# Ninety-six convolution taps on VectorE alone, in a two-layer encoder on one core

## The reference, cut to what matters

```python
def conformer_conv(u, dw_w, dw_b, norm_g, norm_b):
    a, gate = jnp.split(u, 2, axis=-1)
    z = a * jax.nn.sigmoid(gate)
    z = lax.conv_general_dilated(
        z, dw_w[:, None, :].astype(z.dtype), window_strides=(1,),
        padding=[(CONV_PAD, CONV_PAD)], dimension_numbers=('NWC', 'WIO', 'NWC'),
        feature_group_count=CONV_CH) + dw_b      # CONV_CH = 512, 31 taps wide
    z = layer_norm(z, norm_g, norm_b)
    return jax.nn.silu(z)

def attn_conv_mixer(...):
    ...
    attn = block_attention(q, k, v)              # 8 heads, softmax over 512 keys
    conv = conformer_conv(u, dw_w, dw_b, conv_norm_g, conv_norm_b)
    return jnp.concatenate([attn, conv], axis=-1) @ w_out
```

## Time and profile before

| | us |
|---|---|
| median of 3 runs | 1434.68 (1434.39 to 1436.61) |
| the profiled execution, its own time | 1434.18 |
| its span | 1432.4 |
| PE busy | 1383.2 (97%) |
| DVE busy | 664.6 (46%) |
| ACT busy | 459.6 (32%) |
| POOL busy | 221.6 (15%) |

### The profile page before, as it was taken

The page is one execution under the profiler, slowest core; times in us unless marked ns, Lnnn a source line. Parts: engine busy times, 40 slices in busy tenths (PEclk is TensorE's granted clock), DMA queues, the critical chain, the costliest instruction groups (busy, mean ns, idle before and its releaser), DMA issues.

```text
span 1432.4 us, 16564 instructions
## 1 busy us (share of the span) xinstructions
PE 1383.2 (97%) x6684; PEld 1162.5 (81%) x6684; DVE 664.6 (46%) x823; ACT 459.6 (32%) x552; POOL 221.6 (15%) x194
## 2 busy tenths in 40 slices
PE   7969789999999999999999999999999999999997
PEld 7757677888888888889888888888888888888886
DVE  4669893733333322166555453654373333332225
ACT  3357553332232221133232332423233222322211
POOL 5279851300000000033201002000030000000000
PEclk9989999999999999999999999999999999999999
DMA  6200001223222332303231212222222233224221
GB/s 213 89 30 1 30 30 59 89 88 109 96 88 94 109 120 88 115 33 137 67 105 59 88 59 88 89 89 89 88 89 88 88 99 106 88 89 146 88 89 59
DMA packets 84015, 124.15 MB, mean 87 GB/s; under 512 B 2688, under 2 KB 61312, under 8 KB 83968
## 3 DMA queue, kind: packets, MB, share of 16 engines
q1 hardware_dynamic: 83968, 123.49, 25.7%
HBM read 121.39 MB, written 2.10 MB: 86 GB/s over the span
## 4 chain that ended last, share of the span: by engine, by line
PE 86%; DVE 6%; POOL 4%; ACT 2%; issue 1%; DMA 0%; POOLq 0%; DVEq 0%; SPq 0%; ACTq 0%
PE ps L1236 22%; PE ps L1238 22%; PE ps L1237 22%; PE ps L1312 19%; DVE acc L914 2%; POOL acc L501 2%; POOL w_lo L377 1%; PE ps L1249 1%; ACT w_hi L373 1%; DVE row_max L1000 1%; DVE probT_lo L1017 1%; PE ps L1522 0%; PE ps L1442 0%; DMA x_tok<-in_x 0%; DVE x_tok L1059 0%
## 5 line engine op out<-in xcount | busy, mean ns | idle before, releaser
L377 DVE TENSOR_TENSOR w_lo<-raw,w_hi 128x2048 fp32r<-128x2048 f32 x101 | 231.8, 2295 | 487.1 <-ACT w_hi L373 487.1
L1236 PE MATMUL ps<-xT_hi,w_hi 128*128 128x512 f32 (+1 forms) x992 | 366.6, 370 | 0.5 <-POOL w_lo L377 0.5
L1237 PE MATMUL ps<-xT_lo,w_hi 128*128 128x512 f32 (+1 forms) x992 | 365.5, 368 | 0.0
L1238 PE MATMUL ps<-xT_hi,w_lo 128*128 128x512 f32 (+1 forms) x992 | 365.5, 368 | 0.0
L373 ACT ACTIVATE w_hi<-raw 128x2048 fp32r<-128x2048 f32 x109 | 208.4, 1912 | 429.7 <-PE ps L1238 251.1
L1236 PEld LDWEIGHTS ps<-xT_hi,w_hi 128*128 128x128 f32 x992 | 186.9, 188 | 32.1 <-POOL w_lo L377 1.1
L1238 PEld LDWEIGHTS ps<-xT_hi,w_lo 128*128 128x128 f32 x992 | 186.9, 188 | 31.4
L1237 PEld LDWEIGHTS ps<-xT_lo,w_hi 128*128 128x128 f32 x992 | 187.0, 188 | 31.2
L575 POOL TENSOR_SCALAR var_eps<-var_eps 128x1 f32<-128x1 f32 x16 | 5.6, 352 | 846.9 <-ACT squares L768 846.9
L1236 PE MATMUL ps<-w_hi,xT_hi 128*128 128x512 f32 (+1 forms) x320 | 121.3, 379 | 0.0
L1237 PE MATMUL ps<-w_lo,xT_hi 128*128 128x512 f32 (+1 forms) x320 | 121.1, 378 | 0.0
(11 more groups left out here) (167 smaller groups left out, 1760.8 us busy)
## 6 DMA issues: line engine op xcount, KB each, us to landing
raw<-in_l_w_in SPq DMA_DIRECT2D x31, 1024.0 KB, 5.2
raw<-in_l_ffn_w_gate SPq DMA_DIRECT2D x22, 1024.0 KB, 5.1
raw<-in_l_ffn_w_up SPq DMA_DIRECT2D x22, 1024.0 KB, 5.1
raw<-in_l_ffn_w_down SPq DMA_DIRECT2D x22, 1024.0 KB, 4.7
raw<-in_l_w_out SPq DMA_DIRECT2D x12, 1024.0 KB, 4.9
x_tok<-in_x SPq DMA_DIRECT2D x4, 512.0 KB, 7.2
out<-x_tok SPq DMA_DIRECT2D x8, 256.0 KB, 2.1
ln_gb<-in_l_ln_mix_g SPq DMA_DIRECT2D x2, 512.0 KB, 5.2
```

Source lines behind the costliest of these rows:

```text
L377: eng.tensor_tensor(w_lo[ch.s][:], raw[ch.s][:], f32(w_hi[ch.s][:]), ALU.subtract)\
L1236: nc.tensor.matmul(dst, a[0], b[0], start=start, stop=False)
L1237: nc.tensor.matmul(dst, a[0], b[1], start=False, stop=False)
L1238: return nc.tensor.matmul(dst, a[1], b[0], start=False, stop=stop)
```

## The change

All 47 taps that ScalarE and GpSimd shared become VectorE's. `tap_products`, `add_taps`, the buffers `tap_part` and `side_sum` and their semaphores go. VectorE's list of taps is now tiles 0, 1 and 2 in full and the last three taps of tile 3: 96. Ahead of step 0 it does 1 + 19 + 4 of them, and then 3 in every step, which lasts to step 23. PE's wait for the additions in step 27 goes; its own instructions stay the same, in the same order.

```diff
--- before.py
+++ after.py
@@ -76,7 +76,6 @@
-HANDED = 16
...
@@ -87,13 +86,11 @@
-SIDE_SUM_STEP = 25
...
-DVE_TAPS = 2 * TAPS - HANDED + TAPS - BATCH * BATCHES
-ADDED = TAPS - 1 + HANDED - 1
+DVE_TAPS = 3 * TAPS + TAPS - BATCH * BATCHES
...
@@ -489,18 +482,6 @@
-            def add_taps(count):
-                for a in range(added[0], min(added[0] + count, ADDED)):
-                    own_tile = a < TAPS - 1
-                    total = acc[:, 1, :] if own_tile else side_sum[:]
-                    pool.wait_ge(part_tapped, a + (2 if own_tile else 3))
-                    if a:
-                        pool.wait_ge(part_added, a)
-                    nc.gpsimd.tensor_tensor(total, total, tap_part[:, a % 4, :], ALU.add).then_inc(part_added, 1)
-                    added[0] += 1
...
@@ -525,15 +506,9 @@
             for b in range(2):
                 diagonals(b)
-            add_taps(18)
 
             def attention_step(s):
                 b = s // 2
-                add_taps(1 + (s % 4 == 1))
-                if s == SIDE_SUM_STEP:
-                    pool.wait_ge(tap_done, 2 * TAPS - HANDED)
-                    pool.wait_ge(part_added, ADDED)
-                    nc.gpsimd.tensor_tensor(acc[:, 2, :], acc[:, 2, :], side_sum[:], ALU.add).then_inc(part_added, 1)
...
@@ -629,26 +604,6 @@
-            def tap_products(count):
-                for n in range(tapped[0], min(tapped[0] + count, TAPS + HANDED)):
-                    ct, k = (1, n) if n < TAPS else (2, n - HANDED)
-                    tap, z = conv_par[:, ct, k:k + 1], zpad[:, ct, k:k + SEQ]
...
-                        if a >= 4:
-                            act.wait_ge(part_added, a - 3)
-                        nc.scalar.activation(tap_part[:, a % 4, :], z, ACT.Copy, scale=tap).then_inc(part_tapped, 1)
...
@@ -690,9 +645,7 @@
             glu_sigmoid(1)
-            tap_products(16)
             glu_sigmoid(2)
-            tap_products(4)
             glu_sigmoid(3)
...
@@ -709,7 +662,6 @@
                 if s == 0:
                     z_tile_hi()
-                tap_products(1 + (s % 4 == 0))
...
@@ -896,8 +848,8 @@
-            taps = [(0, k) for k in range(TAPS)] + [(2, k) for k in range(TAPS - HANDED)] \
-                + [(3, k) for k in range(BATCH * BATCHES, TAPS)]
+            taps = [(ct, k) for ct in range(3) for k in range(TAPS)] + [(3, k) for k in range(BATCH * BATCHES, TAPS)]
...
@@ -988,9 +940,9 @@
             glu_product(1)
-            conv(9)
+            conv(19)
             glu_product(2)
-            conv(2)
+            conv(4)
...
@@ -1016,7 +968,7 @@
-                conv(2 - s % 2)
+                conv(3)
...
@@ -1447,7 +1399,6 @@
                         pe.wait_ge(tap_done, DVE_TAPS)
-                        pe.wait_ge(part_added, ADDED + 1)
                         pe.wait_ge(conv_copied, 1)
```

More of the change, by code:

```diff
@@ L164, in build_encoder @@
         k_turned = place("k_turned", [P, TT, KV * HD], F32, work + 22 * KB)
-        tap_part = place("tap_part", [P, 4, SEQ], F32, work + 24 * KB)
         qT_hi = place("qT_hi", [P, TT, 4, P], F32R, work + 32 * KB)
@@ L172, in build_encoder @@
         rope_gain = place("rope_gain", [P, TT, 2, 2, HD], F32, work + 68 * KB)
-        side_sum = place("side_sum", [P, SEQ], F32, work + 68 * KB)
         o_raw = [place(f"o_raw{i}", [P, GROUP, 2, HD], F32, work + at * KB) for i, at in enumerate((72, 78))]
@@ L249, in build_encoder @@
         tap_done = sem("tap_done")
-        part_tapped = sem("part_tapped")
-        part_added = sem("part_added")
         diag_made = sem("diag_made")
@@ L489, in _ @@
                             .then_inc(rope_gain_made, 1)
-            added = [0]
-            def add_taps(count):
-                for a in range(added[0], min(added[0] + count, ADDED)):
-                    own_tile = a < TAPS - 1
-                    total = acc[:, 1, :] if own_tile else side_sum[:]
-                    pool.wait_ge(part_tapped, a + (2 if own_tile else 3))
-                    if a:
-                        pool.wait_ge(part_added, a)
-                    nc.gpsimd.tensor_tensor(total, total, tap_part[:, a % 4, :], ALU.add).then_inc(part_added, 1)
-                    added[0] += 1
             for t in range(TT):
@@ L631, in _ @@
             make_hi(act, Chunk(C_Q))
-            tapped = [0]
-            def tap_products(count):
-                for n in range(tapped[0], min(tapped[0] + count, TAPS + HANDED)):
-                    ct, k = (1, n) if n < TAPS else (2, n - HANDED)
-                    tap, z = conv_par[:, ct, k:k + 1], zpad[:, ct, k:k + SEQ]
[L639 to L647, removed]
-                        if a >= 4:
-                            act.wait_ge(part_added, a - 3)
-                        nc.scalar.activation(tap_part[:, a % 4, :], z, ACT.Copy, scale=tap).then_inc(part_tapped, 1)
-                    tapped[0] += 1
             def glu_sigmoid(ct):
@@ L896, in xT_tile_lo @@
                                             f32(xT_hi[spot]), ALU.subtract).then_inc(xT_lo_made, 1)
-            taps = [(0, k) for k in range(TAPS)] + [(2, k) for k in range(TAPS - HANDED)] \
-                + [(3, k) for k in range(BATCH * BATCHES, TAPS)]
+            taps = [(ct, k) for ct in range(3) for k in range(TAPS)] + [(3, k) for k in range(BATCH * BATCHES, TAPS)]
+            assert len(taps) == DVE_TAPS
             tapped = [0]
```

## The result

The changed kernel takes 1447.33 us (median of 6 runs, 1446.52 to 1448.08), the kernel before 1435.51 in 6 runs (1434.39 to 1436.76). The ratio is 1.0082, with an interval of 1.0069 to 1.0095: slower by 11.8 us, where 4.3 were forecast (3.5, if its 1439.0 is set against the 1435.5 of six runs), and above the range's end of 1444.5. The profiled execution took 1448.08 us with a span of 1446.3, against 1434.18 and 1432.4.

The account below looks back on a forecast made before the run. DVE was taken to set the pace in steps 2 to 23, PE from step 24. Start at step 2, 104.8, plus 81.8 and 13.8 put step 24 at 200.4, 4.3 later: 1438.5, so 1439.0; range 1433.5 to 1444.5.

Parts of the forecast that it names:

- The start: Ahead of step 0: PE gets its first scores at 98.3 instead of 106.46, a gain of 8.1 us.
- Steps 0 and 1: Taps, z_lo and 1.7 for GpSimd's first diag_lo and diag; step 2 starts at 104.8, 6.5 us earlier.
- Steps 2 to 23: DVE's pace, 3.69 a step, 81.8 together, plus 13.8 of collisions; step 24 at 200.4, 4.3 us later.
- The collisions: Steps 2 to 23: DVE's taps held up by GpSimd's diagonals, divisions and w_lo; 13.8 us, bounds 6.3 and 24.
- The price of w_lo: Steps 8 and 16: each w_lo catches a tap early, 3.5 and 4.2 us, together 7.7.
- Behind step 24: From step 24 on: nothing differs; the next two steps are PE's in both kernels, 3.92 us.
- The distance from step 24 to the end: Sign for the tail: the same distance as before if the forecast is right.
- Rival 3: Steps 17 to 23 and first PE-bound steps: PE falls to half clock, 1.5 plus 3.4, 4.9 us, 1443.9; chance 0.11.
- Rivals 1 and 2: Steps 2 to 23: first, collisions under 9.5, 1429.8 at lowest bound, 0.07; second, 7 to 12, 1432.2 to 1437.2, 0.22.
- Rival 4: DVE's tap chains: 0.66 a tap, three in 1.98 instead of 2.24; 6.2 us less, 1432.8; chance 0.03.
- Rival 5: DVE's taps stay at 1.4 us, the slowness being their own; +66 us less 8 at the start, 1490; chance 0.01.
- The weighed rule: DVE's taps: 0.61 us for 512 columns, three in 1.83 instead of 2.24, 22 steps save 9 us, near 1430.

Follow-up runs that it names:

- e2: Changed kernel with GpSimd's two w_lo moved from steps 8 and 16 to step 24 and the end of its row; 1439.40 us.
- e1: Changed kernel plus six matmuls nobody reads on PE in each of steps 20 to 24; 1440.30 us.
- e3: Changed kernel with taps alternating between two tiles, each waiting only for its own tile's last tap; 1435.99 us.
- e4: Kernel before, with ScalarE's and GpSimd's early products and additions taken from ahead of step 0 and spread two per step; 1452.12 us.
- e9: Changed kernel plus two matmuls nobody reads on PE in each of steps 20 to 24; 1446.82 us.
- e7: Kernel before, with GpSimd's two w_lo moved from steps 8 and 16 to step 25 and behind the last rsqrt; 1428.84 us.
- e10: Changed kernel with the two w_lo late and six matmuls nobody reads in each of steps 20 to 24; 1434.54 us.
- e5: Changed kernel with the two w_lo late and taps alternating between two tiles; 1425.45 us.

## Why the prediction was wrong, by its own steps

**The start: right.** From the gate product to the first scores 21.79 were forecast (98.3 less 76.51; its own terms, 95.4 and 0.59, 1.30 and 0.92, add up to 98.2), and 21.73 measured (99.78 less 78.05). The taps ahead of step 0 took 0.78 and not 0.79. They are tile 0's, behind the second gate product; the prediction calls them the third tile's, which changes no term.

**Steps 0 and 1: right.** 6.5 forecast from the scores to step 2, 6.54 measured. The first diag_lo and diag cost about what the 1.7 said: three taps were 3.22 (99.39 to 102.61) and z_lo 1.48 (to 104.09), where the forecast had 2.24 and 0.6 without them, so 1.9.

**Steps 2 to 23: right in the sum.** 95.6 forecast (81.8 and 13.8), 95.38 measured. The collisions had been placed by choice between bounds of 6.3 and 24, so a hit this close is in part luck. The price of w_lo was 8.0 (3.8 and 4.2) for 7.7, and e2 gave 7.5 of it back. The rest, diagonals and divisions, is then 5.6 for 6.1, by subtraction. In all of this stretch DVE's maxima waited 0.6 us for PE, as this row of its waits says (total, times, longest):

```profile
DVE row_max L952 <- PE ps L1190: 0.6, 2, 0.4
```

Without the 1.54 of the later start step 24 is at 200.16; 200.4 was forecast.

**Behind step 24: the step that failed.** "Behind step 24 nothing differs: the next two steps are PE's in both, 3.92." Nothing differs in the instructions; the clock did. These two steps took 5.79 (201.70 to 207.49) and the next one 3.84, the half clock held until 221.8, and steps 24 to 30 came out 8.41 longer. The distance from step 24 to the end, which the prediction had named as a sign, is 8.3 longer. Rival 3 had the mechanism and the wrong size: its 4.9 were 1.5 for steps 17 to 23 and 3.4 for two slow steps at the most. The 1.5 did not come at all: the clock was at half from 174 to 194, and DVE's steps there were 3.7 (182.62, 186.31, 189.98). The 3.4 was 8.5. The rows of the kernel before would not have given that. There the clock, once fallen, stayed at 0.50 through 6.00 us of busy PE, which at 3.84 a step is one and a half slow steps, 3 us; the 20.5 us of the kernel after were new. With 8.5 in place of its 4.9, rival 3 gives 1439.0 + 8.5 = 1447.5, beside 1447.33; part of that is luck, since 1439.0 stands on a median of 1434.68, and with 1435.51 it would be 1448.3. What shows the clock as the cause is e1: fillers in steps 20 to 24 alone took 8.0 us off, and steps 24 to 30 back to 16.84.

**The chances.** Rivals 1 and 2 are out: collisions were 13.6 (95.4 less 81.8), and they needed less than 9.5 and 12 at the most. Rival 4 is out for the kernel as it was: 2.23 for three taps. With two chains, in e3, its 0.66 comes true. Rival 5 is out, with a mean of 896 ns. The weighed rule of the Trainium skill (Vector Engine (DVE) Microarchitecture Reference, Measured stream behaviour on trn2), 0.61 us for a tap of 512 columns, is passed by the row in both forms: 0.78 chained, 0.66 in two chains. The second is near it, so most of the gap was the wait of one tap for the other. Its page TensorE: Matmul & The Clock Gate, Part 1, also of the Trainium skill, has activity release the throttle and idleness bring it back, and e1 agrees in direction: PE's steps filled up, 12.00 of 12.00 us, and the clock 1.00 instead of falling.

**What stays open.** What exactly makes the clock fall isn't settled. In the kernel after it was 1.00 from 196.4 to 200 with PE busy 1.80 of 3.60, and fell at about 201.3, 1.6 us after PE had become busy again; two fillers a step changed nothing and six much. Nor is the later fall settled, which every kernel here but the one before has ahead of its output matmuls, though PE stands for probT_lo there in all. In the kernel after, e4 and e9 it comes so late that from the maximum of step 31 to the output they need 11.4 to 11.9 us, against 11.37 before; in the other eight it is 13.7 to 15.1. In e7:

```profile
187.00:207.00 20.00, 17.72 (x132) 15.17 (x130) 16.52 (x36) 11.86 (x26) 11.56 (x10) 1.00 0.17 53
208.00:220.00 12.00, 11.81 (x57) 11.52 (x56) 4.40 (x8) 5.19 (x8) 8.59 (x7) 0.50 0.01 2
```

Without it e1 and e10 would win some 3 us more (31.1 and 31.4 against 28.3). And that e3's and e5's short runs have a short tail is inferred from their times and mean clocks.

## What to carry to other kernels

Moving work onto the engine that paces a stretch has a second price, the clock of the engine that it starves; read what the granted clock does at the place where TensorE becomes the bound again, and give its length a wide range: one fallen clock lasted 6 us of busy PE in the kernel before, and 20 in the kernel after. Where an engine is the pace, look first at what collides with it: the two late w_lo gave 8 to 9 us on either kernel for a move of two instructions, against 11.8 that the change lost. A chain of dependent vector instructions in two interleaved chains costs 0.66 apiece instead of 0.79.

## What the runs showed of the hardware that was not expected

- Work that nobody reads made the kernel faster: 30 matmuls in steps 20 to 24 took 8.0 us off the time (e1), ten took nothing (e9).
- The clock went to 0.50 when PE had been busy again for 1.6 us, and not in the idle steps ahead of it (1.00 from 196.4 to 200), and stayed there for 20.5 us with PE busy 19.46 of it.
- In the kernel before, the same clock stood at 1.00 through the whole tail (28.28), although it had been at 0.50 from 182 to 188.
- Runs of one kernel fall into groups, which is more than scatter: e3 at 1434.2, 1436 and 1442.4; e5 at 1425 and 1432; the kernel before at 1434.4, 1436.7 and 1438.5. The mean clock of a long run is lower (0.983 at 1438.5, 0.989 at 1434.4 in the kernel before).
